# Stage edges of a two-block transformer kernel cut by row tile and column half, with the modulation sums taken there

## The reference, cut to what matters

```python
shift, scale, gate = modulation(c, ada_w[layer, 0], ada_b[layer, 0])
h = x * (1.0 + scale) + shift
y = hybrid_mixer(h, ...)
x = layer_norm(DN_ALPHA * x + (1.0 + gate) * y, post_ln_g[layer, 0], post_ln_b[layer, 0])
...
h = rms_norm_2(x, norm_ffn[l]) * (1 + sc_f) + sh_f
x = x + g_f * ((jax.nn.silu(h @ w_gate[l]) * (h @ w_up[l])) @ w_down[l])
```

## Time and profile before

| What | Value |
|---|---|
| median of 3 runs | 2231.6 us (2228.99 to 2235.2) |
| the profiled execution | 2228.76 us |
| its span in the profile | 2227.0 us |
| mean granted clock of TensorE | 0.943 |
| TensorE busy | 2009.0 us, 90% |
| VectorE busy | 1686.4 us, 76% |
| moved by DMA | 554.39 MB, mean 249 GB/s |

### The profile page before, as it was taken

How to read it: one execution, slowest core, us unless ns; L and a number is a source line. 1 busy time by engine, 2 the same in 40 slices (tenths; PEclk the granted TensorE clock), 3 DMA queues, 4 the chain that set the end, 5 groups by cost and what they waited for, 6 DMA issues and landing times.

```text
span 2227.0 us, 28329 instructions
## 1 busy us (share of the span) xinstructions
PE 2009.0 (90%) x11552; PEld 1736.1 (78%) x11552; DVE 1686.4 (76%) x1768; ACT 1163.7 (52%) x1248; POOL 72.4 (3%) x121
## 2 busy tenths in 40 slices
PE   6878899888779999999999999878879998978998
PEld 6676899777567887888788788667669997857997
DVE  6764888876468989898899988887768886675444
...
GB/s 351 227 161 133 245 336 352 296 126 95 132 185 331 355 359 369 330 351 375 345 337 363 368 332 353 308 128 181 92 93 351 329 347 165 114 76 107 178 188 95
DMA packets 250922, 554.39 MB, mean 249 GB/s; under 512 B 10044, under 2 KB 75824, under 8 KB 250784
## 3 DMA queue, kind: packets, MB, share of 16 engines
...
q10 hardware_dynamic: 268, 0.07, 0.0%
HBM read 551.40 MB, written 1.05 MB: 248 GB/s over the span
## 4 chain that ended last, share of the span: by engine, by line
PE 70%; DVE 16%; ACT 7%; issue 4%; DMA 3%; SPq 0%; DVEq 0%; ACTq 0%
PE bank L471 21%; PE bank L473 20%; PE bank L472 20%; DVE ring_lo L1825 4%; ACT ring_hi L1184 2%; PE bank L825 1%; DVE acc L1776 1%; DMA ring<-in_w_in_dram 1%; DMA ring<-in_ffn_w_dram 1%; PE bank L542 1%; DMA ring<-in_ada_w_dram 1%; PE bank L1011 1%; PE bank L525 1%; DVE XN L2047 1%; DVE hT L1880 1%
## 5 line engine op out<-in xcount | busy, mean ns | idle before, releaser
L1825 DVE TENSOR_TENSOR ring_lo<-ring,ring_hi 128x2048 fp32r<-128x2048 f32 x417 | 950.3, 2287 | 267.8 <-ACT ring_hi L1184 264.9
L1184 ACT ACTIVATE ring_hi<-ring 128x2048 fp32r<-128x2048 f32 x417 | 795.8, 1914 | 492.5 <-PE bank L473 237.2
L471 PE MATMUL bank<-hh,ring_hi 128*128 128x256 f32 x1152 | 332.7, 289 | 21.6 <-DVE ring_lo L1825 9.7
L472 PE MATMUL bank<-hl,ring_hi 128*128 128x256 f32 x1152 | 330.4, 287 | 0.0
L473 PE MATMUL bank<-hh,ring_lo 128*128 128x256 f32 x1152 | 330.1, 287 | 0.0
L471 PE MATMUL bank<-ring_hi,hh 128*128 128x256 f32 (+2 forms) x672 | 221.4, 329 | 29.3 <-DVE hl L1884 8.9
L471 PEld LDWEIGHTS bank<-hh,ring_hi 128*128 128x128 f32 x1152 | 225.6, 196 | 26.5 <-issue 11.5
L473 PE MATMUL bank<-ring_hi,hl 128*128 128x256 f32 (+2 forms) x768 | 244.4, 318 | 0.0
L1776 DVE SCALAR_TENSOR_TENSOR acc<-ring,csil,acc 128x1024 f32<-128x1024 f32 x180 | 231.2, 1284 | 13.9 <-DMA ring<-in_ada_w_dram 8.4
L471 PE MATMUL bank<-ring_hi,hgh 128*128 128x512 f32 (+1 forms) x576 | 220.2, 382 | 7.8 <-DVE ring_lo L1825 3.1
L472 PEld LDWEIGHTS bank<-hl,ring_hi 128*128 128x128 f32 x1152 | 225.8, 196 | 0.7 <-issue 0.2
...
## 6 DMA issues: line engine op xcount, KB each, us to landing
...
```

The source lines that it names most:

```text
L471: pe.matmul(ps, xh, wh, start=first, stop=False)
L472: pe.matmul(ps, xh, wl, start=False, stop=False)
L1184: act.activation(ring_hi[i % NH][:, 0:z], ring[n % NS][:, 0:z], ACT.Copy).then_inc(*s.hi(("hi", home(s, i), i)))
L1825: dve.tensor_tensor(ring_lo[n % NS][:, 0:z], ring[n % NS][:, 0:z], hi, ALU.subtract).then_inc(*s.lo(("lo", home(s, i), i)))
```

## The change

The last two weight blocks of each stage are multiplied by tile and half: (0,0), (0,1), (1,0), (1,1), each with its own signal. Residual, statistics or squares follow by half; tile 0 is normalized between the two halves of tile 1. In the second model the square root of a tile follows its own squares. The output leaves in four transfers instead of two. For m = 1, 2, 3, 5, 6, 7 shift and scale are no longer summed inside the stage before, but both at the edge, right behind the last products (`together`), copied out of PSUM by ScalarE into `both`, and turned into `cols` by VectorE after it has normalized tile 1. The accumulators of m = 2 and m = 6 move into YT and QK, the modulation blocks of m = 4 come ahead of those of m = 2 in the list, and the gates of m = 6 and 7 are summed in stage 6. The experts' second block is split after edge 3 instead of ahead of it, and at edge 4 one block's low half goes behind the normalization.

```diff
@@ -126,6 +126,7 @@
         pB = sb("pB", [128, 36])
         pD = sb("pD", [128, 80])
         lnc = sb("lnc", [128, 8])
+        both = sb("both", [128, 16])
         warm = sb("warm", [128, 1])
         csil = sb("csil", [128, 16])
         small = sb("small", [128, 2, 24])
@@ -255,7 +256,17 @@
             return acc[:, 1024 * j:1024 * j + 1024]
 
 
-        ED = [[v.rearrange("p (h l) -> p h l", h=8) for v in pair] for pair in ((gate[1][:, :], gate[2][:, :]), (acc_of(0), acc_of(1)))]
+        ED = [[v.rearrange("p (h l) -> p h l", h=8) for v in pair] for pair in ((gate[1][:, :], gate[2][:, :]), (gate[0][:, :], gate[1][:, :]))]
+
+        def sums_at(m, j):
+
+            if m == 2 and j < 2:
+                return YTf[:, 1024 * j:1024 * j + 1024], None
+            if m == 6:
+                return QKf[:, 1024 * j:1024 * j + 1024], None
+            order = [0, 1, 4, 3, 5, 7] if j < 2 else [0, 1, 2, 3, 4, 5, 7]
+            i = order.index(m)
+            return acc_of(j), (order[i - 1], j) if i else None
 
 
         plan, where = [], {}
@@ -338,7 +349,7 @@
 
         WHOLE = [("wout", l, i) for l in range(2) for i in (2, 3)]
         put_blocks(weave(ffn_blocks((("ffn", 0), a["ffn_w1"][0], a["ffn_w3"][0], a["ffn_w2"][0])),
-                         mods((1, 2), (2, 0), (2, 1), (2, 2), (3, 0), (3, 1), (4, 0), (4, 1))))
+                         mods((1, 2), (4, 0), (4, 1), (2, 0), (2, 1), (2, 2), (3, 0), (3, 1))))
         put_blocks(weave(win_blocks(1) + rowblocks(("wout", 1), a["w_out"][1]), mods((3, 2))))
         put_blocks(weave(ffn_blocks(*[(("moe", x), a["moe_w1"][0, x], a["moe_w3"][0, x], a["moe_w2"][0, x]) for x in range(8)]), mods((4, 2)), 6, 6))
         IN_MOE = [(4, 2)]
@@ -360,10 +371,17 @@
                ("wout2", 0, 3), ("ffn2", 0, "w2", 10), ("wout2", 1, 3), ("ffn2", 1, "w2", 10)]
 
         sums = {}
+
+        TOGETHER = (1, 2, 3, 5, 6, 7)
         for m in range(8):
             for j in range(3):
                 if (m, j) == (0, 2):
                     sums[turn_of["win", 0, 1024]] = [(0, 2)]
+                    continue
+                if m in TOGETHER and j < 2:
+                    continue
+                if j == 2 and m >= 6:
+                    sums.setdefault(turn_of[("win2", 1, 2) if m == 6 else ("wout2", 1, 1)], []).append((m, j))
                     continue
                 n = where["mod", m, j, 3]
                 i = 2 + next((turn_of[k] for k, _ in plan[n:] if k in turn_of), len(split))
             for k in range(i + 2, i + look + 1):
-                if k >= len(split) or (split[k][0:2] != split[i][0:2] and split[k][0] in ("win", "ffn", "win2", "ffn2")):
+                if k >= len(split) or (split[k][0:2] != split[i][0:2] and split[k][0] in ("win", "ffn", "win2", "ffn2", "moe")):
                     return min(k - 1, len(split) - 1)
             return min(i + look, len(split) - 1, moe0 + EARLY - 1 if i < moe0 else len(split))
+            def together(m):
+
+                ps = psum("together", m)
+                for j in range(2):
+                    pe.wait_ge(*at("acc", m, j))
+                    for i in range(8):
+                        x = pe.matmul(ps[:, 8 * j + i:8 * j + i + 1], sums_at(m, j)[0][:, 128 * i:128 * i + 128], ones[:, 0:1], start=True, stop=True)
+                x.then_inc(*main.small(("sum", m, 0), ("sum", m, 1)))
+
             def to_features(key, src, ready, steps=range(4)):
-                ban = {kk: psum(*key, kk) for kk in steps}
+                ban = {}
                 for t in range(2):
                     for name in ready[t]:
                         pe.wait_ge(*at(*name))
                     for kk in steps:
+                        if t == 0:
+                            ban[kk] = psum(*key, kk)
...
                 for t in range(2):
-                    for i in blocks:
-                        if t == 0:
-                            pe.wait_ge(*at("y", name, l, i))
-                        x = out_products(name, l, i, t, False, i == blocks[-1])
-                        if t:
-                            x.then_inc(*main.prod(("use", "main", (name, l, i)), ("Y", name, l, t)))
-                        elif i == blocks[-1]:
-                            x.then_inc(*main.prod(("Y", name, l, t)))
+                    for h in range(2):
+                        for i in blocks:
+                            if t == 0 and h == 0:
+                                pe.wait_ge(*at("y", name, l, i))
+                            wh, wl = weights(main, name, l, i)
+                            for k in range(2):
+                                kc, z, c = 2 * i + k, slice(128 * t, 128 * t + 128), slice(1024 * k + 512 * h, 1024 * k + 512 * h + 512)
+                                x = product(Y[t][h][:, :], hh[:, kc, z], yl[:, kc, z], wh[:, c], wl[:, c], False, i == blocks[-1] and k == 1)
+                            if i == blocks[-1]:
+                                x.then_inc(*main.prod(("Y", name, l, t, h), *([("use", "main", (name, l, i))] if t and h else [])))
+                            elif t and h:
+                                x.then_inc(*main.prod(("use", "main", (name, l, i))))
...
+                for t in range(2):
+                    for hf in range(2):
+                        for i in (9, 10):
+                            wh, wl = weights(s, *key, "w2", i)
+                            g, h = divmod(i, 2)
+                            if t == 0 and hf == 0:
+                                pe.wait_ge(*at(s.part, *key, "u", g, h))
+                            for c in range(2):
+                                w = slice(1024 * c + 512 * hf, 1024 * c + 512 * hf + 512)
+                                j, z = 2 * h + c, slice(128 * t, 128 * t + 128)
+                                x = product(Y[t][hf][:, :], fuh[g % 2][:, j, z], ful[g % 2][:, j, z], wh[:, w], wl[:, w], False, i == 10 and c == 1)
+                            names = [("use", s.part, (*key, "w2", i)), (s.part, *key, "down", i, 1)] if t and hf else []
+                            if i == 10:
+                                names.append((s.part, *key, "result", t, hf))
+                            if names:
+                                x.then_inc(*s.prod(*names))
 
...
+            def together(m):
+                if m in TOGETHER:
+                    act.wait_ge(*at("sum", m, 1))
+                    act.activation(both[:, :], R.of("together", m)[:, 0:16], ACT.Copy).then_inc(*main.act(("sums", m), ("free", "together", m)))
+
             def layer_norm(i):
                 roots_next()
                 for t in range(2):
                     sd(("ln", i, t), stat(4, "ln", i)[:, 2 * t + 1:2 * t + 2])
+                together(i)
...
             def rms_rows(m, ready):
                 roots_next()
+                ss = stat(4, "rms", m)
                 for t in range(2):
-                    for z in ready[t]:
-                        act.wait_ge(*at(*z))
-                    act.activation(XN[:, t, :], X[:, t, :], ACT.Square, accum_out=stat(2, "rms", m)[:, t:t + 1]).then_inc(*main.act(("rms", m, t)))
-                for t in range(2):
-                    sd(("rms", m, t), stat(2, "rms", m)[:, t:t + 1])
+                    for h in range(2):
+                        c = slice(512 * h, 512 * h + 512)
+                        act.wait_ge(*at(*ready(t, h)))
+                        act.activation(XN[:, t, c], X[:, t, c], ACT.Square, accum_out=ss[:, 2 * t + h:2 * t + h + 1]).then_inc(*main.act(("rms", m, t)))
+                    sd(("rms", m, t), ss[:, 2 * t:2 * t + 1])
+                together(m)
...
-                        c = 18 * ((m - 4) // 2) + 8 * (m % 2)
-                        dve.wait_ge(*at("pB"))
-                        x = dve.scalar_tensor_tensor(cols[:, m, 8:16], ps[:, 0:8], 1.0, pB[:, c:c + 8], ALU.add, ALU.mult)
-                    x.then_inc(*vec(("cols", m, j), ("free", "sum", m, j)))
+                    columns_of(m, j, R.of("sum", m, j))
+                    main.vec.when["free", "sum", m, j] = main.vec.last()
+
+            def together(m):
...
@@ -1861,13 +1932,19 @@
                     settled()
                     dve.tensor_tensor(X[:, t, :], X[:, t, :], rows[:, 1, :], ALU.add).then_inc(*vec(("x", i, t)))
 
-            def rms_rows(m):
-                ss = stat(2, "rms", m)
-                for t in range(2):
-                    dve.wait_ge(*at("rms", m, t))
-                    rstd(("rms", m, t), ss[:, t:t + 1], 1024, 1e-6)
-                    settled()
-                    dve.tensor_scalar(XN[:, t, :], X[:, t, :], ss[:, t:t + 1], None, ALU.mult).then_inc(*vec(("n", m, t)))
+            def mean_square(m, t):
+                ss = stat(4, "rms", m)
+                dve.wait_ge(*at("rms", m, t))
+                dve.tensor_tensor(ss[:, 2 * t:2 * t + 1], ss[:, 2 * t:2 * t + 1], ss[:, 2 * t + 1:2 * t + 2], ALU.add).then_inc(*vec())
+                settled()
```

(71 more changed lines are left out.)

138 lines of the change are left out of this document (65 added, 73 removed).

## The result

The changed kernel takes 2205.9 us (median of 4 runs, 2200.9 to 2206.3) against 2230.9 of the kernel before (4 runs): a ratio of 0.988, 95% interval 0.986 to 0.990. It is faster, by 25.0 us. The forecast was 2196, with a range of 2184 to 2214: the sign and the range held, the size was 10 us too large.

The account below looks back on a forecast made before the run. TensorE's work plus its pauses at the seven edges was taken as the bound. Edges and end 21.4 us plus stages 14.0 make 35.4 off 2228.8, 2193.4; with 2.8 from profiled execution to median, 2196, range 2184 to 2214.

Parts of the forecast that it names:

- So the sums are hidden at full clock: Edges 1 and 2: TensorE's 32 added matmuls end about when VectorE is ready; without that cover an edge loses 3.6 us.
- the rival with the sums on the path: At the edges: slow sums delay TensorE, the edges give -2.9 us and the stages 14, time 2220; chance 0.08.
- the refills at "nothing": GpSimd's queue: the m = 4 refill waits for edge 1's sums, but VectorE wants it some 15 us later; no cost.
- The clock stays up: Rival: slow first products after edges 2, 3, 5 and the router run at full rate, about 8 us more, 2188; chance 0.13.
- The halves: Work by half at the edges: 2.2 us each at edges 1 and 2, 2.4 each at edges 5 to 7.
- with no backlog: Edges 1 and 2: if VectorE had no backlog, each would gain 2.9 us instead of 2.2.
- Edge 3: The low half leaves and VectorE works off parts sooner; TensorE's sums and tile 0 end at 591.2, leaving 8.1 us gain.
- Stages: Stage 5 gains 7.5 us, stage 1 3.5, stage 0 2.8, stages 2 and 4 1.2, stage 6 loses 1.0; together 14.0.
- The experts: no loss, the slower case: Experts stage: 268 loads each 0.13 us longer would take all 35 us, 0.3 longer would give 2240; chance 0.04.
- the rival by which the stages keep their time: Stages 1 and 5: the DMA takes their gain of 11.0 us, time 2207; chance 0.17.
- The end: Program end: one half residual fewer behind the last product, 1.3 us gained; the smaller last transfer counted as nothing.
- the halves do nothing: Rival: VectorE is still behind at every edge; edge 3 keeps 2.3 us, the stages stay, time 2212; chance 0.03.

Follow-up runs that it names:

- run 4: Changed kernel with the gates' sums of m = 6 and 7 placed by the general rule again, as in the kernel before; 2203.6 us, ratio 0.9878.
- run 2: Changed kernel with the shift and scale sums back in the stages, as in the kernel before, halves and moved block kept; 2210.6 us, ratio 0.9914.
- run 8: Changed kernel with two unread 128x496 products behind each 16 matmuls of the sums at the edges; 2214.9 us, ratio 0.9915.
- run 11: Changed kernel with GpSimd's refills held until the last hT of edges 1 and 5, second sample; 2205.5 us, ratio 0.9874.
- run 1: Kernel before with only the experts' second block split later, behind edge 3; 2229.0 us, ratio 0.9989.
- run 6: Changed kernel with the last products by whole tile and then block, all else still by half; 2219.2 us, ratio 0.9937.

## Why the prediction was right in sign and range, and 10 us too far

**The step that failed is "So the sums are hidden at full clock", taken as the price at every edge.** At full clock they are hidden but for 0.3 us (edge 6: 4.65 with them, 4.34 without; edge 3 in run 4: 4.67, where the prediction had about 5), but the edges are not at full clock throughout. At edges 2, 3 and 7 the clock fell 3.2, 2.0 and 2.3 us behind the last product, in the middle of the sums; 32 took 3.8, 4.9 and 4.5 us, the 16 transposes 3.5 to 3.65, and TensorE's own chain set `hT`. The text named what a loss of the cover costs and left it out of the sum; the rival with the sums on the path had 0.08 and 2220, and a part of it came true. At edges 1 and 5 the sums were in time, but GpSimd's refills came to lie on VectorE's last instructions, released by the sums at edge 1 and by the last product at edge 5: 1.1 and 1.7 us. The text had put the refills at "nothing", by who waits for them and not by what they lie beside. Both together cost 6.4 to 8.0 us (run 2 against the changed kernel's two profiles).

**The clock stays up** did not come true for the changed kernel: its clock falls 2.0 to 5.2 us behind the last product, that of run 2, without sums at the edges, 4.3 to 5.4. At edge 7 it fell at 2.3 to 2.4 in five of the six profiles with halves and all the sums there and at 4.0 in the sixth (run 8 with its added products aside), at 4.2 to 5.8 in the six without. It is no fixed rule: at edge 3 of runs 4 and 11, with the same sums, the clock stayed at 1.00 for 8.7 and 8.8 us. The Trainium skill, "TensorE: Matmul & The Clock Gate", Part 1, says that activity releases the throttle; in the windows of edge 7 above TensorE is busy for 2.00 of 2.00 us with the sums, and the clock falls all the same: from that sentence alone the fall does not follow.

**The halves** were under-priced in sum: 2.2 at the layer norm edges and 2.4 at the others, where without the sums they give 1.5, 2.8, 1.8 and three times 3.3 (run 1 against run 2). Edge 2 came near the prediction's 2.9 "with no backlog", edges 5 to 7 above their upper bound of 2.7, edge 1 below the value taken.

**Edge 3**, 8.1 forecast: 6.2 and 7.6 in the two profiles. The block has 5.8 of it; the halves add 1.8 where no sums are in the way.

**The two parts compete for one pause.** With the block moved in all four: neither 2229.0 (run 1), the halves alone 2210.6, the sums alone 2219.2, both 2206.1. At the edges this is plain: the six take 45.2 us with neither, 45.5 with the sums alone, 29.2 with the halves alone and 37.2 and 35.5 with both. So the sums cost 0.3 us where the edge is long, and 6.4 to 8.0 beside the halves. The times go the same way (the sums gain 9.8 us alone and 4.5 beside the halves, the halves 18.4 and 13.1), but these medians come from two batches, by the ratios it is 11.6 and 8, 16.7 and 13, and with the intervals as they are the times alone would not prove it. (Run 6 keeps the residuals by half and run 1 the gates of before, so the four are not quite pure.) The forecast added the gain of the sums in the stages and that of the halves at the edges as if each had the edge to itself.

**Stages.** Stage 5: 8.5 for 7.5, and runs 2 and 4 tie it to the sums and the gate (203.9 with both back, 198.3 with the gate back). Stage 0: 2.0 for 2.8. Stage 1: 1.5 for 3.5, as TensorE's waits grew. Before, it waited 8.5 us for low halves and 0.5 for the gated product; after, by the view of its waits in stage 1 (us, times, longest):

```profile
PE bank L489 <- DVE ring_lo L1897: 7.9, 5, 3.9
PE bank L489 <- DVE PTr L2036: 4.0, 1, 4.0
```

That is 2.9 us more, at a DMA share of 0.84 as before: a part of the rival by which the stages keep their time, in stage 1 only. Stage 6: 2.9 lost for 1.0: the two gates cost their whole time, and the gate that left the stage's start had stood beside the splitting of `h`. Stages 2 and 4: 1.2 forecast, nothing found. The experts: no loss, the slower case had nothing in it. The end: 1.3, confirmed by run 6.

**Two rivals' times** do not follow from the prediction's own terms: "the halves do nothing" comes to 2214 (2231.6 less 2.3, 0.4, 1.3 and 14), not 2212, and 268 loads at 0.3 us more each to 80 us and so about 2276, not 2240. For edge 3 the rows give 7.8 rather than 8.1, since TensorE's 591.2 lies 0.7 behind the end of the scaling. None of this changes the forecast by more than 0.3.

**In sum**: 19.7 forecast for the six edges, 13.7 and 15.3 measured in the two profiles; 15.7 for the rest, 8.9 and 7.6 measured. The total is nearer than its terms: without the sums in the way the six edges gain 21.7 (before against run 2), 2.0 more than forecast, and this hid a part of what the sums cost there.
